# Attention of a two-layer trunk: query tiles 4 to 7 by pairs, with the values as fp32r high and low columns

## The chip, the core and the metric

The kernel runs on one core of a Trainium2 chip. The metric is the device time of one launch in microseconds (us), lower is better. The program's engines are named as in the profile: PE is TensorE, DVE is VectorE, ACT is ScalarE, POOL is GpSimd, SP is SyncE, which here only issues DMAs.

## The reference

The model has two layers over x (1 x 1024 x 1024, float32): an even one with latent attention beside an S5 state-space branch, and an odd one with chunked gated linear attention. Each ends in x <- LayerNorm(alpha * x + y). The change lies in the even layer and at its end:

```python
def block(args):                       # 8 blocks of 128 queries, 8 heads, q and k of 64 + 32, v of 64
    qn, qp, i = args
    s = (jnp.einsum('bqhd,bkhd->bhqk', qn, k_nope)
         + jnp.einsum('bqhr,bkr->bhqk', qp, k_pe)).astype(jnp.float32) * scale
    causal = k_idx[None, :] <= q_idx[:, None]
    s = jnp.where(causal, s, -jnp.inf)
    p = jax.nn.softmax(s, axis=-1).astype(v.dtype)
    return jnp.einsum('bhqk,bkhd->bqhd', p, v)

y = jax.nn.gelu(y)                                      # s5_layer, 256 wide
y = y * jax.nn.sigmoid(y @ w_glu + b_glu)

o_mla = mla_attention(...) * jax.nn.silu(g_mla)         # even_layer, 512 wide
o_s5 = s5_layer(...) * jax.nn.silu(g_s5)
return jnp.concatenate([o_mla, o_s5], axis=-1) @ w_out
```

All inputs and the output are float32.

## The kernel before

All 1024 tokens are cut in 8 tiles of 128 (P = 128, NT = 8). TensorE has two kinds of product here. An fp32 product is one instruction that the hardware runs as passes of its own. An "fp32r" product uses operands that were split beforehand in a high part (a copy rounded to fp32r) and a low part (raw minus high), and three passes: hi x hi, lo x hi, hi x lo. The big projections are of the second kind; the attention's scores, transposes and values are of the first.

Attention goes through `heads`, 64 pairs (i, h) of query tile and head, tile by tile. For each, with i + 1 blocks of 128 keys:
- "s": scores. TensorE multiplies the turned queries of the head (qTt, 96 x 128, as weights) with the turned keys kT, up to 512 columns per instruction, and adds the causal mask (L1963, L1967). Tiles 0 to 3 use one of four PSUM banks, tiles 4 to 7 two pairs of banks in turn.
- VectorE takes the negative maximum out of PSUM (negmax, L1623), ScalarE the exponential with the row sum as accumulator (prob, L1209).
- "pt": TensorE transposes prob block by block (L1885) into banks 4 and 5, at most four blocks a bank. VectorE copies the first bank of a head to SBUF, ScalarE the second one (both `copy_probs`, L696), into four slots of probT.
- "av": TensorE multiplies with probT as weights and 64 columns of V as the moving operand (L2100), into bank 7, where the 8 heads of a tile lie side by side.

At a tile's last head VectorE takes the reciprocals of the sums (L1682), scales the output (L1684) and multiplies the gate (L1688, into the gate's own buffer). "OT": TensorE transposes the gated tile, and VectorE copies it to OT (L1691). "q" and "qT" compute and transpose the queries of later tiles in between; GpSimd turns their rotary part.

Beside it VectorE computes the sigmoid of the S5 gate in 16 pieces (`sigmoid_gate`, L1646 to L1648: 1 + exp, reciprocal, product; the exponentials ran on ScalarE), and GpSimd splits w_out (rows 128 k, k = 0 to 5): k = 1 to 3 while the queries of tiles 2 to 4 pass, k = 0, 4, 5 behind tile 7's, then w_gk and the first head of wqk, a weight of the next layer.

Then the output projection: "z0" for tile i multiplies the split w_out with the mixed tile (4 blocks of OT, 2 of gs5), whose high parts ScalarE casts (`mix_hi_tile`, L1228, L1229) and whose low parts VectorE subtracts (`mix_lo_tile`, L1654, L1656). For each tile the layer norm follows: VectorE adds the residual and takes the statistics, ScalarE the root, GpSimd applies ln_g and ln_b (L1030, L1031), TensorE turns the result (zn). The transposes of tile 7's gated output, "OT" of tile 7, stand after the product of tile 0.

The order of the work on every engine is the order in which `attention_steps` yields its steps; each engine's program walks through the same list and takes its own part of each step. A plan hands PSUM banks from job to job: a job claims its bank when the reader of the job before has freed it, and "filled" and "drained" are waits on the semaphores of a job's writer and reader. SP's DMAs stand in one list too; each waits for what frees its buffer.

## Time and profile before

| | |
|---|---|
| median of 3 runs | 893.23 us (891.41 to 896.03) |
| the profiled execution | 895.35 us, span of its core 893.3 us, mean granted clock 0.986 |
| PE busy | 852.8 us, 95% of the span, 4360 instructions |
| DVE busy | 590.0 us, 66% |
| ACT busy | 326.9 us, 37% |
| POOL busy | 248.1 us, 28% |
| DMA | 64.21 MB, mean 72 GB/s |

The span is the time between the first and the last instruction of the profiled execution; the time of the execution lies 2.1 us above it. Matmuls overlap in a trace: a row's duration is longer than the distance to the next one's start, and it is the distance that tells the engine's rate. The granted clock is given as a share of full speed, 2.4 GHz; the engine's other level is 1.2 GHz. A row with xN stands for N instructions that follow one another. L12 is line 12 of the kernel.

### The profile page before, as it was taken

What the parts mean: (1) busy time and instruction counts of PE and PEld (TensorE: products, weight loads), DVE (VectorE), ACT (ScalarE), POOL (GpSimd) and SP (SyncE); (2) the same over time, 40 slices, a digit from 0 to 9 for tenths busy, and PEclk for the clock granted to TensorE, in tenths of its full rate; (3) what the DMA queues carried; (4) which work ended last, traced back from release to release, by engine and by line L of the source; (5) the groups of instructions that cost most, each with busy time, mean ns of one, the idle gap of its engine ahead of it and who ended that gap; (6) DMA issues with size and microseconds to landing.
All of it is one profiled execution on the core that took longest, in us unless ns stands there. A gap on an engine that the chain in (4) does not pass through costs nothing.

```text
span 893.3 us, 12333 instructions
## 1 busy us (share of the span) xinstructions
PE 852.8 (95%) x4360; PEld 691.8 (77%) x4360; DVE 590.0 (66%) x961; ACT 326.9 (37%) x626; POOL 248.1 (28%) x251
## 2 busy tenths in 40 slices
PE   7999999999999999999998999999799999999995
PEld 5899777756677777787875888888588888888884
DVE  6988688557687775637871443488986667544543
ACT  6251514654333434412222645045243446111210
POOL 2000001415211111506656231005753013332243
PEclk9999999999999999999998899999999999999998
DMA  9101164220000111032223110236334322111111
GB/s 335 35 20 30 48 118 96 50 74 1 1 2 1 39 34 48 1 105 108 95 95 118 47 48 1 83 94 191 123 102 140 105 74 103 38 61 48 48 59 59
DMA packets 40685, 64.21 MB, mean 72 GB/s; under 512 B 8256, under 2 KB 21824, under 8 KB 40608
## 3 DMA queue, kind: packets, MB, share of 16 engines
q1 hardware_dynamic: 40624, 63.42, 23.2%
q8 instruction: 35, 0.57, 0.3%
q14 instruction: 26, 0.21, 0.1%
HBM read 52.33 MB, written 9.44 MB: 69 GB/s over the span
## 4 chain that ended last, share of the span: by engine, by line
PE 72%; DVE 17%; ACT 3%; DMA 3%; issue 2%; SPq 1%; POOL 1%; DVEq 0%; ACTq 0%; POOLq 0%
PE psum L1876 39%; PE psum L2177 14%; PE psum L2100 6%; PE psum L1963 6%; PE psum L1885 6%; PE psum L1911 1%; DVE vg_lo L1748 1%; DVE probT L696 1%; DMA wgs_raw<-even_w_in_dram 1%; DVE x_hi_raw L1779 1%; DVE x_lo_raw L1780 1%; DMA xT_raw<-x_cols_dram 1%; DMA ln_gb<-ln_b_dram 1%; DVE qTt L1617 1%; ACT xT_hi L1117 1%
## 5 line engine op out<-in xcount | busy, mean ns | idle before, releaser
L2177 PE MATMUL psum<-vg_hi,x1T_hi 128*128 128x512 f32 x208 | 82.0, 394 | 4.9 <-DVE vg_lo L1748 4.2
L2177 PE MATMUL psum<-vg_hi,x1T_lo 128*128 128x512 f32 x208 | 81.7, 393 | 0.0
L2177 PE MATMUL psum<-vg_lo,x1T_hi 128*128 128x512 f32 x208 | 81.6, 392 | 0.0
L2100 PEld LDWEIGHTS psum<-V,probT 128*128 128x128 f32 x576 | 69.3, 192 | 12.4 <-issue 8.4
L1209 ACT ACTIVATE prob<-psum,negmax 128x128 f32<-128x128 f32 (+7 forms) x64 | 47.4, 741 | 82.0 <-DVE negmax L1623 74.4
L2100 PE MATMUL psum<-V,probT 128*128 128x64 f32 x576 | 74.5, 275 | 0.5 <-DVE rot L1684 0.3
L1963 PE MATMUL psum<-kT,qTt 96*128 96x512 f32 (+3 forms) x192 | 72.5, 487 | 1.2 <-DVE YT L713 1.2
L1623 DVE TENSOR_REDUCE negmax<-psum 128x1 f32<-128x128 f32 (+7 forms) x64 | 48.5, 758 | 28.2 <-PE psum L1967 26.7
L696 DVE COPY probT<-psum 128x512 f32<-128x512 f32 (+3 forms) x64 | 37.8, 591 | 22.4 <-PE psum L1885 20.7
L2177 PEld LDWEIGHTS psum<-vg_hi,x1T_hi 128*128 128x128 f32 x208 | 39.3, 189 | 15.3 <-DVE vg_lo L1748 6.2
L1876 PE MATMUL psum<-x1T_lo,wqk_hi 128*128 128x512 f32 x128 | 50.8, 397 | 0.0
L1876 PE MATMUL psum<-x1T_hi,wqk_hi 128*128 128x512 f32 x128 | 50.8, 397 | 0.0
L1876 PE MATMUL psum<-x1T_hi,wqk_lo 128*128 128x512 f32 x128 | 50.8, 397 | 0.0
L1876 PE MATMUL psum<-w_out_hi,Y1T_hi 128*128 128x512 f32 x128 | 50.6, 395 | 0.0
L1876 PE MATMUL psum<-w_out_hi,Y1T_lo 128*128 128x512 f32 x128 | 49.9, 390 | 0.0
L1876 PE MATMUL psum<-w_out_lo,Y1T_hi 128*128 128x512 f32 x128 | 49.8, 389 | 0.0
L1963 PEld LDWEIGHTS psum<-kT,qTt 96*128 96x128 f32 x192 | 32.4, 190 | 20.0 <-issue 16.8
L2177 PEld LDWEIGHTS psum<-vg_hi,x1T_lo 128*128 128x128 f32 x208 | 39.4, 189 | 8.3
L2177 PEld LDWEIGHTS psum<-vg_lo,x1T_hi 128*128 128x128 f32 x208 | 39.3, 189 | 8.1
L1399 DVE SCALAR_TENSOR_TENSOR SG<-V,psum 128x512 f32<-128x512 f32 x16 | 11.0, 688 | 49.8 <-PE psum L1876 49.8
L1096 POOL TENSOR_TENSOR SG<-SG,ln_gb 128x1024 f32<-128x1024 f32 (+1 forms) x8 | 18.2, 2277 | 92.1 <-DVE SG L1406 92.1
L1885 PE MATMUL psum<-ident,prob 128*128 128x128 f32 x288 | 42.4, 274 | 0.8 <-ACT prob L1209 0.5
(393 smaller groups left out, 2087.5 us busy)
## 6 DMA issues: line engine op xcount, KB each, us to landing
vg_piece<-odd_w_in_dram SPq DMA_DIRECT2D x60, 256.0 KB, 3.3
wqk_raw<-odd_w_in_dram SPq DMA_DIRECT2D x8, 512.0 KB, 5.3
x_res<-x_dram SPq DMA_DIRECT2D x8, 512.0 KB, 4.0
x_scratch<-zn SPq DMA_DIRECT2D x8, 512.0 KB, 2.9
w_out_raw<-odd_w_out_dram SPq DMA_DIRECT2D x4, 1024.0 KB, 5.0
V<-x_scratch SPq DMA_DIRECT2D x8, 512.0 KB, 4.4
out_dram<-SG SPq DMA_DIRECT2D x8, 512.0 KB, 2.9
xT_raw<-x_cols_dram SPq DMA_DIRECT2D x7, 512.0 KB, 7.6
```

Of the source, the lines that this page charges most:

```text
L696: ins = engine.activation(dst, src, ACT.Copy) if engine is nc.scalar else engine.tensor_copy(dst, src)
L1096: step(pool.tensor_tensor(z, z, g, ALU.mult))
L1117: step(act.activation(xT_hi[:, k, s], xT_raw[k][:, s], ACT.Copy), xT_hi_set)
L1209: step.frees(act.activation(prob[:, place:place + (i + 1) * P], src, ACT.Exp, bias=negmax[:, n % 4:n % 4 + 1], accum_out=rsum[:, i % 2, h: ...
L1399: step.frees(vec.scalar_tensor_tensor(zt[:, s], res[:, s], ALPHA, bank(job, i, n), ALU.mult, ALU.add), (job, i, n))
L1617: step.frees(vec.tensor_copy(qTt[:, n % 2, 4 * half:4 * half + 4, :], bank("qT", n, half)[0:QK, :].rearrange("p (h t) -> p h t", h=4)), (" ...
L1623: step(vec.tensor_reduce(negmax[:, n % 4:n % 4 + 1], scores(n)[0], AX_X, ALU.max, negate=True), max_set)
L1876: mm = pe.matmul(out, lhsT, rhs, start=(k == 0), stop=(k == len(pairs) - 1))
L1885: mm = pe.transpose(bank(*job)[0:rows, k * P:k * P + cols], block_in, identity[0:cols, 0:cols])
L1963: mm = pe.matmul(psum[:, slot + part, 0:c1 - c0], qTt[:, i % 2, h, :], kT[:, h, c0:c1], start=True, stop=not diag, skip_group_check=diag)
L2100: mm = pe.matmul(bank("o", i)[:, h * VD:(h + 1) * VD], lhsT, rhs, start=(k == 0), stop=(k == len(pairs) - 1))
L2177: mm = pe.matmul(bank(*job), lhsT, rhs, start=(k == 0 and j == 0 and product not in ADDS_TO), stop=(k == 3 and j == len(pairs) - 1), skip_ ...
```

## The change

For query tiles 4 to 7 the list `heads` now takes two tiles together: (4,0), (5,0), (4,1), (5,1) and so on, then tiles 6 and 7. A pair (tile 2p, tile 2p+1) of one head is a step m. Its probabilities are transposed as before, but each transposed bank is split in fp32r: ScalarE casts the high part (L1304), VectorE subtracts the low part from PSUM (L1777). Both tiles' blocks of the same keys stand side by side in a cell (hi and lo, 4 blocks x 2 tiles x 128 queries); there are three cells. "pv" replaces "av": the weights are 128 columns of V, the head's 64 value columns as fp32r high parts and the same 64 as low parts, and the moving operand is 256 columns of the cell, first the high ones, then the low ones. So two passes a block give (hi + lo) x (hi + lo), with the high columns' product in one half of the partitions and the low columns' in the other; ScalarE copies one half out (`output_parts`), VectorE adds them (`output_gated`). The last block of a pair serves the second tile alone, with 128 columns. The output comes out turned (value x query), so the tile is not transposed; instead the gate is: VectorE scales the gate by the reciprocals of the sums (`gate_scaled`), TensorE transposes it ("gT"), ScalarE copies it to gateT, and VectorE multiplies. This happens once for every two heads of a pair of tiles.

V is stored per block of keys as [high | two raw or low columns | high] (V_raw names the middle as float32). GpSimd casts the high columns of all blocks behind the turning of tile 2's queries, with the low columns of blocks 4 to 7 there, and the low columns of blocks 0 to 3 once tile 3's last values are done. The first pv waits for them.

Tiles 0 to 3 go one by one as before, but VectorE alone copies their probT. Further:
- ScalarE computes the S5 gate's sigmoid by its own function; VectorE multiplies it in four pieces at heads 10 to 16.
- The queries of tiles 4 to 7 are computed and transposed at other steps (QUERIES, TURNS), with a second buffer qt.
- GpSimd splits w_gk and then the six pieces of w_out in one block behind tile 7's queries; wqk's first head is loaded at the end of the attention and split between the layer norms of tiles 2 and 3. ln_g and ln_b are loaded behind it, once the last output is gated.
- "OT" of tile 7 behind the first product is gone.

The diff, cut to its core:

```diff
-        heads = [(i, h) for i in range(NT) for h in range(H)]
+        heads = [(i, h) for i in range(4) for h in range(H)]
+        FIRST = len(heads)
+        heads += [(2 * p + t, h) for p in range(2, NT // 2) for h in range(H) for t in range(2)]
...
             for n, (i, h) in enumerate(heads):
+                if n > FIRST and n % 2 == 0 and n > FIRST + 1:
+                    yield "pv", (n - FIRST) // 2 - 1
                 yield "pt", n
...
-                if n:
+                if 0 < n <= FIRST:
                     yield "av", n - 1
-                if h == 4 and i:
+                if n < FIRST and h == 4 and i:
                     yield "OT", i - 1
-            yield "av", len(heads) - 1
+                if n == FIRST + 2:
+                    yield "OT", 3
+                if n in OUTPUT_TURNS:
+                    yield "gT", OUTPUT_TURNS.index(n)
+            yield "pv", STEPS - 1
+            yield "gT", PAIRS - 1
             yield "z0", 0
-            yield "OT", NT - 1
...
# ScalarE, at "pt"
-                    if 4 <= n + 1 < len(heads):
+                    if 4 <= n + 1 < len(heads) and (n < FIRST or n % 2 == 0):
                         exponentials(n + 1)
-                    for number, first, blocks in pt_jobs[heads[n]][1:]:
-                        copy_probs(act, step, number, first, blocks)
+                    for number, first, blocks in pt_jobs[heads[n]] if n >= FIRST else ():
+                        plan.filled(act, ("pt", number))
...
+                        (hi, _), source = prob_blocks(n, number, first, blocks)
+                        step(act.activation(hi, source, ACT.Copy), prob_hi_set)
+                    if FIRST < n + 1 < len(heads) and n % 2:
+                        exponentials(n + 1)
+                    if n in OUTPUT_TURNS:
+                        output_parts(OUTPUT_TURNS.index(n))
...
# VectorE, at "pt"
+                    if n in OUTPUT_TURNS:
+                        gate_scaled(OUTPUT_TURNS.index(n))
+                    if n - 1 in OUTPUT_TURNS:
+                        output_gated(OUTPUT_TURNS.index(n - 1))
...
+                            vec.wait_ge(prob_hi_set, number + 1 - FIRST)
+                            (hi, lo), source = prob_blocks(n, number, first, blocks)
+                            step.frees(vec.tensor_tensor(lo, source, hi.bitcast(F32), ALU.subtract), ("pt", number))
-                    if 24 <= n < 56 and n % 2 == 0:
-                        sigmoid_gate((n - 24) // 2)
+                    if n in (10, 12, 14, 16):
+                        sigmoid_gate((n - 10) // 2)
...
# TensorE
+                elif what == "pv":
+                    p, h = 2 + n // H, n % H
+                    job = ("o_odd" if h % 2 else "o_even", n // 2)
...
+                    for k in range(2 * p + 2):
...
+                        t0 = int(k == 2 * p + 1)
+                        for part, cell in enumerate(cells[(2 * n + k // 4) % 3]):
+                            mm = pe.matmul(bank(*job)[:, c0 + t0 * P:c0 + 2 * P],
+                                           V[k][:, h // 2, 2 * (h % 2):2 * (h % 2) + 2, :].rearrange("p s d -> p (s d)"),
+                                           cell[:, k % 4, t0:2, :].rearrange("p t q -> p (t q)"),
...
+    def gate_scaled(j):
+        p, k = 2 + j // 4, j % 4
+        plan.drained(vec, ("s", FIRST + 4 * j + 3))
...
+        step(vec.reciprocal(inverses, sums))
+        block_ = gate[:, k, 2 * p * P:2 * (p + 1) * P].rearrange("p (t h d) -> p t h d", t=2, h=2)
+        step(vec.tensor_tensor(block_, block_, inverses.unsqueeze(3).to_broadcast([P, 2, 2, VD]), ALU.mult), gated)
+
+    def output_gated(j):
+        p, k = 2 + j // 4, j % 4
+        plan.drained(vec, ("o_even", j))
+        src = bank("o_odd", j)
+        step(vec.tensor_tensor(o_sum[0:VD, :], src[0:VD, 0:2 * P], o_low[0:VD, :], ALU.add))
+        step(vec.tensor_tensor(o_sum[VD:P, :], src[VD:P, 2 * P:4 * P], o_low[VD:P, :], ALU.add))
+        plan.drained(vec, ("gT", j))
+        step.frees(vec.tensor_tensor(OT[:, k, 2 * p * P:2 * (p + 1) * P], o_sum[:, :], gateT[j % 2][:, :],
+                                     ALU.mult), ("o_odd", j))
...
# GpSimd
-                if 2 <= i < 5:
-                    w_out0_split_slice(i - 1, 0, 48)
+                if i == 2:
+                    for j in (4, 5, 6, 7, 0, 1, 2, 3):
+                        plan.drained(pool, ("vp", j))
+                        step(pool.tensor_copy(V[j][:, :, 0:4:3, :], V_raw[j][:, :, 1:3, :]))
+                        if j >= 4:
+                            value_low(j)
+                if i == 5:
+                    plan.filled(pool, ("o", 3))
+                    for j in range(4):
+                        value_low(j)
...
+                if i in (2, 3):
+                    wqk_split_part(0, i - 2)
...
# SP, at tile 1 of the output projection's residual loads
-                    sp.wait_ge(gated, NT)
+                    plan.filled(sp, ("o_odd", PAIRS - 1))
+                    wqk_load(0)
+                    plan.drained(sp, ("o_odd", PAIRS - 1))
```

How this moves instructions, first on ScalarE in tile 7 of the kernel before. An exponential and one copy of a bank follow each other, head by head:

```order
L1209 ACTIVATE prob,rsum<-psum,negmax 128x1024
L696 ACTIVATE probT<-psum 128x384
L1209 ACTIVATE prob,rsum<-psum,negmax 128x1024
L696 ACTIVATE probT<-psum 128x512
L1209 ACTIVATE prob,rsum<-psum,negmax 128x1024
L696 ACTIVATE probT<-psum 128x512
L1209 ACTIVATE prob,rsum<-psum,negmax 128x1024
```

And on ScalarE in the pair of tiles 6 and 7 now, from the exponential of tile 6's head (896 columns) on; probT_hi_89, 91 and 93 are the three cells:

```order
L1262 ACTIVATE prob,rsum<-psum,negmax 128x896
L1262 ACTIVATE prob,rsum<-psum,negmax 128x1024
L1304 ACTIVATE probT_hi_89<-psum 128x4x128
L1304 ACTIVATE probT_hi_91<-psum 128x3x128
L1286 ACTIVATE o_low<-psum 64x256
L1287 ACTIVATE o_low<-psum 64x256
L1315 ACTIVATE gateT_204<-psum 128x256
L1304 ACTIVATE probT_hi_89<-psum 128x4x128
L1304 ACTIVATE probT_hi_91<-psum 128x4x128
L1262 ACTIVATE prob,rsum<-psum,negmax 128x896
L1262 ACTIVATE prob,rsum<-psum,negmax 128x1024
```

Two exponentials stand together now, four copies of high parts behind them, of which in every second step two are preceded by the output's three copies.

On VectorE in tile 7 before, with tile 6's normalisation in the middle:

```order
L1623 TENSOR_REDUCE negmax<-psum 128x1
L696 COPY probT<-psum 128x512
L1623 TENSOR_REDUCE negmax<-psum 128x1
L1682 RECIPROCAL rinv<-rsum 128x8
L1684 TENSOR_TENSOR rot<-psum,rinv 128x512
L1688 TENSOR_TENSOR gate<-gate,rot 128x512
L696 COPY probT<-psum 128x512
L1623 TENSOR_REDUCE negmax<-psum 128x1
```

And on VectorE in tiles 6 and 7 now, a step with output work (probT_lo_90, 92 and 94 are the cells' low parts):

```order
L1698 TENSOR_REDUCE negmax<-psum 128x1
L1727 RECIPROCAL rinv<-rsum 128x2x2
L1729 TENSOR_TENSOR gate<-gate,rinv 128x256
L1777 TENSOR_TENSOR probT_lo_90<-psum,probT_hi_89 128x4x128
L1777 TENSOR_TENSOR probT_lo_92<-psum,probT_hi_91 128x3x128
L1698 TENSOR_REDUCE negmax<-psum 128x1
L1737 TENSOR_TENSOR o_sum<-psum,o_low 64x256
L1738 TENSOR_TENSOR o_sum<-psum,o_low 64x256
L1740 TENSOR_TENSOR gate<-o_sum,gateT_204 128x256
L1777 TENSOR_TENSOR probT_lo_90<-psum,probT_hi_89 128x4x128
L1777 TENSOR_TENSOR probT_lo_92<-psum,probT_hi_91 128x4x128
L1698 TENSOR_REDUCE negmax<-psum 128x1
```

A head's single copy has become two subtractions, which stand between the maxima; the scaling of the gate stands before the first head's, the gating of the output before the second head's.

On GpSimd before, from the last turning of queries (qt) to the first layer norm (zn):

```order
L706 TENSOR_TENSOR qt<-work 128x8x16
L993 CAST w_out_hi<-w_out_raw_184 128x1024
L994 TENSOR_TENSOR w_out_lo_190<-w_out_raw_184,w_out_hi 128x1024
L993 CAST w_out_hi<-w_out_raw_188 128x1024
L994 TENSOR_TENSOR w_out_lo_194<-w_out_raw_188,w_out_hi 128x1024
L993 CAST w_out_hi<-w_out_raw_189 128x1024
L994 TENSOR_TENSOR w_out_lo_195<-w_out_raw_189,w_out_hi 128x1024
L993 CAST w_gk<-w_gk_raw 128x8x16
L994 TENSOR_TENSOR w_gk<-w_gk_raw,w_gk 128x8x16
L993 CAST wqk_hi<-wqk_raw 128x1024
L994 TENSOR_TENSOR wqk_lo<-wqk_raw,wqk_hi 128x1024
L993 CAST wqk_hi<-wqk_raw 128x1024
```

And now, from the same place, the rows from the fourth piece of w_out on:

```order
L1026 CAST w_out_hi<-w_out_raw_213 128x1024
L1027 TENSOR_TENSOR w_out_lo_219<-w_out_raw_213,w_out_hi 128x1024
L1026 CAST w_out_hi<-w_out_raw_214 128x1024
L1027 TENSOR_TENSOR w_out_lo_220<-w_out_raw_214,w_out_hi 128x1024
L1026 CAST w_out_hi<-w_out_raw_209 128x1024
L1027 TENSOR_TENSOR w_out_lo_215<-w_out_raw_209,w_out_hi 128x1024
L1079 TENSOR_TENSOR zn<-zn,ln_gb 128x512
L1080 TENSOR_TENSOR zn<-zn,ln_gb 128x512
L1079 TENSOR_TENSOR zn<-zn,ln_gb 128x512
```

The split of wqk no longer stands ahead of the layer norms of tile 0; the pieces of w_out are six in a row.

## Rows read from the trace of the kernel before

**Rows 1.** The page, part 4: the last chain, its share of the span by engine.

```profile
PE 72%; DVE 17%; ACT 3%; DMA 3%; issue 2%; SPq 1%; POOL 1%; DVEq 0%; ACTq 0%; POOLq 0%
```

**Rows 2.** Windows: us; busy us (instructions) of PE, PEld, DVE, ACT, POOL; PEclk; DMA; GB/s.

```profile
262.70:388.10 125.40, 124.96 (x839) 99.08 (x839) 88.69 (x125) 50.63 (x102) 23.53 (x24) 1.00 0.09 28
407.40:463.90 56.50, 56.50 (x266) 46.55 (x267) 42.06 (x64) 13.61 (x27) 37.99 (x28) 0.97 0.29 103
```

**Rows 3.** Timeline of PE in tile 7: start us, us, engine line op out<-in xcount.

```profile
359.30 1.88 PE L1963 MATMUL psum<-kT,qTt 96*128 96x512 f32 x4
361.07 1.95 PE L2100 MATMUL psum<-V,probT 128*128 128x64 f32 x16
362.86 1.05 PE L1885 MATMUL psum<-ident,prob 128*128 128x128 f32 x8
363.74 1.88 PE L1963 MATMUL psum<-kT,qTt 96*128 96x512 f32 x4
...
365.46 0.22 PE L1967 MATMUL psum<-causal_bias,ident_b 128*128 128x128 bf16 x1
```

**Rows 4.** Chain of waits in tile 4 (281 to 294 us): start us, us, what.

```profile
282.34 1.08 PE psum L1963 x4
...
283.48 1.11 PE psum L2100 x10
```

**Rows 5.** Timeline of PE in the input projection, two passes 32 apart.

```profile
83.75 0.35 PE L1911 MATMUL psum<-wa_hi,xT_lo 128*128 128x416 f32 x1
...
89.73 0.34 PE L1911 MATMUL psum<-wa_lo,xT_hi 128*128 128x416 f32 x1
```

**Rows 6.** Timeline of ACT in tile 7.

```profile
363.59 1.11 ACT L1209 ACTIVATE prob<-psum,negmax 128x1024 f32<-128x1024 f32 x1 [3.32 <-DVE negmax L1623]
...
364.82 0.60 ACT L696 ACTIVATE probT<-psum 128x512 f32<-128x512 f32 x1
```

**Rows 7.** Timeline of DVE in tile 7; in brackets idle us before, releaser.

```profile
362.28 1.23 DVE L1623 TENSOR_REDUCE negmax<-psum 128x1 f32<-128x1024 f32 x1
363.56 0.69 DVE L696 COPY probT<-psum 128x512 f32<-128x512 f32 x1
365.79 1.22 DVE L1623 TENSOR_REDUCE negmax<-psum 128x1 f32<-128x1024 f32 x1 [1.54 <-PE psum L1967]
```

**Rows 8.** DVE's groups by form: xcount | busy us, mean ns | idle us before, releaser.

```profile
L1647 DVE RECIPROCAL SGL<-SGL 128x128 f32<-128x128 f32 x16 | 15.2, 953 | 0.6
L1623 DVE TENSOR_REDUCE negmax<-psum 128x1 f32<-128x768 f32 x8 | 7.7, 958 | 3.5 <-PE psum L1967 3.3
```

**Rows 9.** ACT's groups by form.

```profile
L1209 ACT ACTIVATE prob<-psum,negmax 128x768 f32<-128x768 f32 x8 | 7.2, 902 | 17.0 <-DVE negmax L1623 17.0
```

**Rows 10.** POOL's groups by form.

```profile
L994 POOL TENSOR_TENSOR w_out_lo<-w_out_raw,w_out_hi 128x1024 fp32r<-128x1024 f32 x6 | 14.1, 2352 | 0.5
L994 POOL TENSOR_TENSOR wv_lo<-wv_raw,wv_hi 128x512 fp32r<-128x512 f32 x4 | 5.1, 1274 | 0.3
```

**Rows 11.** One line, L1688: xcount, ns shortest/median/longest, first and last start us, forms.

```profile
L1688 DVE TENSOR_TENSOR gate<-gate,rot x8: 692/693/1746, 206.9 to 389.8; 128x512 f32<-128x512 f32 x8
```

**Rows 12.** Timeline of ACT: end of tile 0, and output projection.

```profile
197.87 0.49 ACT L1182 ACTIVATE qt<-psum 128x384 f32<-128x384 f32 x1 [3.81 <-PE psum L1876]
...
401.24 1.28 ACT L1251 ACT_TABLE_LOAD   x1 [15.81 <-DVE stat L1403]
```

**Rows 13.** Timeline of DVE at the output projection's start.

```profile
397.06 0.69 DVE L1691 COPY OT<-psum 128x512 f32<-128x512 f32 x1 [6.55 <-PE psum L1885]
```

**Rows 14.** Timeline of POOL there.

```profile
405.98 1.32 POOL L1031 TENSOR_TENSOR zn<-zn,ln_gb 128x512 f32<-128x512 f32 x1
```

**Rows 15.** Timeline of PE there.

```profile
407.36 0.66 PE L1885 MATMUL psum<-ident,zn 128*128 128x128 f32 x4 [2.19 <-POOL zn L1031]
```

**Rows 16.** DMA issues: out<-in queue op xcount, KB each, median us to landing.

```profile
wqk_raw<-odd_w_in_dram SPq DMA_DIRECT2D x8, 512.0 KB, 5.3
ln_gb<-ln_b_dram SPq DMA_DIRECT2D x2, 512.0 KB, 6.0
```

More of the change, by code:

```diff
@@ L211, in hybrid_trunk @@
         prob = at("prob", D1, [P, 2 * S])
-        probT = at("probT", RD + 17920, [P, 4, 512])
+        cells = [[at(f"probT_{part}{c}", RD + 14336 + 2048 * c + 1024 * n, [P, 4, 2, P], F32R)
+                  for n, part in enumerate(("hi", "lo"))] for c in range(3)]
         cT = at("cT", D2, [P, 3, S])
@@ L465, in hybrid_trunk @@
                 count += 1
+        STEPS = (len(heads) - FIRST) // 2
+        PAIRS = STEPS // 2
+        cell_users = [(m, g) for m in range(STEPS) for g in range(2)]
         SHORT = [n for n, (i, h) in enumerate(heads) if i < 4]
@@ L1950, in queries_turn @@
                 pe.wait_ge(q_turned, n + 1)
-                turned(("qT", n, half), [(qt[:, h, :], QK) for h in range(4 * half, 4 * half + 4)])
+                turned(("qT", n, half), [(qt[n % 2][:, h, :], QK) for h in range(4 * half, 4 * half + 4)])
             def score(n):
```

207 lines of the change are left out of this document (135 added, 72 removed).

## The prediction, made before the changed kernel was run

> **What bounds the kernel now.** I read the chain of waits first: TensorE holds 72% of it [rows 1], so the question is where an instruction of TensorE can be saved and who is late when it is. Then the stages: from the first transposes of query tile 4 (262.7 us) to the first product of the output projection (388.1) TensorE is busy 124.96 of 125.40 us, VectorE 88.69, ScalarE 50.63 [rows 2]. One head of tile 7 shows why. Scores begin at 359.30, values at 361.07, transposes of the next head at 362.86, the next scores at 363.74 [rows 3]: 1.77 + 1.79 + 0.88 = 4.44 us without a gap. The values are 8 blocks of 0.224 us, each two passes with the probabilities as weights and 64 columns moving; the transposes are 0.11 us a block. A head of tile 4 has 1.08 us of scores and 1.11 us of values [rows 4], that is 0.215 and 0.222 us a block; the mask between them costs 0.06. So a head of tile 4, 5, 6, 7 takes 2.75, 3.3, 3.9, 4.45 us, and two heads 6.16 us (tiles 4 and 5) or 8.35 us (6 and 7). Eight of each are 116.1 us; four halves of queries (5.2), six of their transposes (2.6) and the transposes of outputs (1.8) bring it to 125.7, as measured.
>
> **The values on TensorE.** 128 heads' worth of blocks go: 8 x (5+6+7+8) = 208 of 0.224 us, 46.6 us. In their place a pair of tiles shares each block of values: two passes, high and low probabilities, over 256 columns, and the last block two over 128. An f32r pass over 416 columns takes (89.73 - 83.75)/32 = 0.187 us [rows 5], 0.0135 more than 416/2.4 GHz; by the same surplus 256 columns take 0.120. No row has f32r with so few columns. From below it is bounded by the 0.112 us of a value pass now [rows 3], from above by what an fp32 product over 256 columns takes, 2 x 0.215 = 0.43 [rows 4]. I take 0.120, since the 416-column row is of the same kind, and 0.11 for 128 columns. A round (one head of both tiles) then costs TensorE, scores + transposes + values: tiles 4, 5: 2.49 + 1.21 + 1.42 = 5.12 us; tiles 6, 7: 3.34 + 1.65 + 1.90 = 6.89 us. Were TensorE still the bound, 8 x (1.04 + 1.46) = 20 us would be won.
>
> **What is late next.** The order of the changed kernel shows a ring through VectorE and ScalarE. ScalarE runs both exponentials of a round, then four copies of high parts; VectorE runs low(first tile), maximum, low(second tile), maximum. The exponential of the second tile waits for VectorE's last maximum, the high copies stand behind it, and the low parts behind them. Durations [rows 6 to 9]: exponential over 1024 columns 1.11, with its accumulator read 1.23 to the next instruction's start (363.59 to 364.82), over 768 by the same 0.12 about 1.02; a copy over 512 0.60; a maximum 1.23 (1024) and 0.96 (768), so 0.27 us per 256 columns; a low part out of PSUM 0.69 (512), and 0.56, 0.42, 0.29 for three, two, one blocks by that slope. A VectorE step costs 0.04 more to the next. Between engines I read 0.08 (maximum ends 363.51, exponential starts 363.59) and 0.27 from TensorE's issue to a reader (the mask's at 365.46 + 0.06, the maximum at 365.79).
> With A the end of the second maximum, tiles 6, 7: exponential A+0.08 to 1.31, high part to 1.91, low part 1.99 to 2.68; second group 2.72 to 3.28; maximum over 896 from 3.32; the second tile's two low parts 4.45 to 5.87 (its transposes could start at 2.76, its high part ends at 4.05, so they are ready); its successor's scores end on TensorE at 3.80 + 1.77 = 5.57, readable at 5.85; maximum 5.91 to 7.14. **7.14 us a round** against 8.35 before. Tiles 4, 5: low part ends 2.47, one-block low part and maximum over 640 to 3.70, but the second tile's high part is there only at 2.47 + 0.08 + 0.44 + 0.25 + 0.60 + 0.08 = 3.92; low parts to 5.11, maximum over 768 to **6.07 us a round** against 6.16. TensorE (5.12, 6.89) waits inside both rings.
> The sum from tile 4's first transposes:
> - 8 rounds of 6.07 and 7 of 7.14, and 0.6 for the first maxima of tiles 6, 7: 99.2 us.
> - Output steps, after every second round. ScalarE's two partial copies and the gate copy fit beside VectorE; the reciprocal and scaling of the gate fit in VectorE's 2 us of waiting after A. Three VectorE steps over 256 columns (3 x 0.46 = 1.38) do not: they stand before the second tile's low parts. Three times 1.38 - 0.22 and four times 1.38: 9.0 us.
> - Four copies of turned queries on VectorE, 0.73 each: 2.9 us.
> - The start. Tile 3's normalisation (about 1.8 us on VectorE) falls in round 1: +1.6. In round 2 two halves of queries (1.29 each) and tile 3's output transposes stand before scores, and the first values wait for four low parts of GpSimd, 1.27 us each [rows 10], that begin when tile 3 is done: +3.1. Together 4.7.
> - Low parts of the first two mixes (0.73 + 0.42 each), hidden under TensorE before: 2.3 us.
> - From A of the last round to the first output product: low part at 4.8, values 1.9, gate transposes 0.2: 7.0 us.
> - VectorE's SBUF steps beside GpSimd: 0.9 us. The row is tile 6's gate product, which took 1.75 us while GpSimd split weights; the median of the eight is 0.69 [rows 11].
> Sum 126.0 against 125.4: **+0.6 us**. The 20 us stay in the waits.
> The Trainium skill (SBUF — State Buffer, section "SBUF: two separate sides") speaks against this change more strongly: a VectorE step with two SBUF inputs and a GpSimd step shut each other out of a shared port for a whole instruction. The trace agrees as far as it goes, with the one product of 1.75 us. By the rule every output step during the six weight splits, now one block of about 21 us (w_out_lo 2.35 each), could wait up to 2.35 us [rows 10]; some three output rounds lie there, so the sum would be up to 5 us higher instead of 0.9.
>
> **Before and after that stage.** The gate of the S5 branch becomes a Sigmoid: two table loads of 1.28 us each [rows 12]. The first lies in the time in which ScalarE waits for TensorE's products, the second before the exponential of head 4, where ScalarE had idled 3.81 us [rows 12]: cost 0.1 (at most 2.6). Sixteen reciprocals of 0.95 us leave VectorE [rows 8]; TensorE waited for few of them, since the stage of tiles 0 to 3 gives VectorE short copies, and what turns up there is paid back by tile 5's queries, whose turning moves into it. I take 0 for tiles 0 to 3, bounds -2 and +2.6.
> At the projection's start the kernel now turns tile 7's output after the first product: VectorE copies it at 397.06 [rows 13] before the layer norm may begin, a table load at 401.24 follows [rows 12], GpSimd ends at 407.30 [rows 14], and TensorE, 2.19 us idle, restarts at 407.36 [rows 15], 19.3 us after 388.1. After this wait the granted clock falls: over the 56.5 us from 407.4 it is 0.97, over the attention before it 1.00 [rows 2]. That is a few us at the lower of its two levels, 1.2 instead of 2.4 GHz, and costs 0.03 x 56.5 = 1.7 us; the two decimals allow 1.4 to 2.0, I take 1.5. In the changed kernel the output tile needs no turning there, so VectorE starts when the first half of the product is ready: 8.3 (product) + 2.1 (VectorE) + 1.7 (ScalarE with its table load) + 1.1 + 3.1 (GpSimd) = 16.3 us, when TensorE has just ended the second product at 16.5 us: no wait, no slow passes. **-4.3 us**. It needs ln_gb: issued about 2.3 us after the first product's start behind a megabyte of wqk (landings 6.0 and 5.3 us) [rows 16], so there at about 12, wanted at 13. The split of wqk's first head, moved among the layer norms of tiles 2 and 3 (3.5 us each), fits: GpSimd has 5.3 us of work in 9.1 us a tile.
>
> Sum: 0.6 - 4.3 = -3.7 us. The profiled execution took 895.35 us (span 893.3 and 2.1 around it), so it would take 891.6; it lies 2.1 above the median of the three runs, 893.23, and from that I forecast **889.5 us**.
>
> **Rivals.**
> 1. TensorE stays the bound. For it: it is busy in 99% of the stage, and my ring has sixteen hand-overs estimated to a tenth. If they close faster, rounds cost 5.2 and 7.0, the output steps hide, and the stage ends at about 8 x 12.2 + 7.4 (queries) + 5 (start, tail) = 110: -15 and -4.3, 874 us; half of it gives 882. Against it: VectorE's own four steps and ScalarE's exponential are rows.
> 2. Slower: the clock. In an output round of tiles 4, 5 TensorE idles 6.07 + 1.16 - 5.23 = 2.0 us, as long as the wait of 2.19 us after which it fell [rows 15]; one fall costs 1.5 us, and if it comes back into each of some ten such rounds the stage gains 15 us: 889.5 + 15 = 904. It decides once one wait is as long as that one. Against it: the 2.0 us are spread over two or three waits.
> 3. An f32r pass over 256 columns costs more. From 0.17 us on TensorE's round of tiles 6, 7 passes the ring with its output steps; at 0.215 the stage takes 129 us (893 in all), at 0.43 it takes 170 (934).
> 4. ln_gb or the GpSimd queue is late and the projection starts no sooner: 893.5 us.
>
> **How the numbers follow.** Forecast 0.54, its own range 885 to 895; rival 1 0.24; rival 2 0.12; rival 3 0.05; rival 4 0.05. About 0.5% (4.5 us, below 888.8 or above 897.7) is what a measurement can tell. Faster: 0.24 and 0.21 of the forecast's own, 0.45. Slower: 0.12 and 0.03 of rival 3, 0.15. The rest, 0.40, is the same. Range 876 to 901: below it lies the full form of rival 1, above it the full form of rival 2 and rival 3.
>
> **What would show it.** In the changed trace: value passes 0.12 us apart; in rounds of tiles 6, 7 about 7.1 and 8.5 us in turn, in tiles 4, 5 about 6.1 and 7.2; TensorE waiting for probT low parts and prob, VectorE idle about 2 us before the first low part of a round; the first transposes of zn 16.5 us after the first product, with clock 1.00. I am wrong if TensorE is 98% busy in the stage (rival 1), if its clock is below 0.95 there (rival 2), or if passes stand 0.17 us apart or more (rival 3).

## The result, and the profile after

The changed kernel took 899.58 us in the median of 6 runs (897.23 to 902.61), the kernel before 895.11 us beside it: 1.0053 times, 95% interval 1.0032 to 1.0074. It is 0.5% slower, where 889.5 us and "the same or faster" were forecast. The profiled execution took 902.61 us, span 900.9, mean granted clock 0.98 (before: 895.35, 893.3, 0.986).

What the ring through VectorE and ScalarE was said to cost came out nearly to the digit. This is a round of tiles 6 and 7 without output steps, then one with them, on VectorE (start us, us, line, operation; in brackets idle time before, and what ended it):

```profile
352.69 1.28 DVE L1777 TENSOR_TENSOR probT_lo<-psum,probT_hi 128x512 fp32r<-128x512 f32 x2 [2.02 <-ACT probT_hi L1304]
...
356.59 1.22 DVE L1698 TENSOR_REDUCE negmax<-psum 128x1 f32<-128x1024 f32 x1
...
362.28 0.42 DVE L1737 TENSOR_TENSOR o_sum<-psum,o_low 64x256 f32<-64x256 f32 x1
...
365.10 1.22 DVE L1698 TENSOR_REDUCE negmax<-psum 128x1 f32<-128x1024 f32 x1
```

The second maximum ends at 357.81 and at 366.32; the one before, 2.02 us ahead of 352.69, at 350.67: rounds of 7.14 and 8.51 us, forecast 7.14 and 8.5. The same ring on ScalarE: the exponential begins 0.08 us after 357.81, the high parts follow it at 359.13, and VectorE's low part follows them at 359.83:

```profile
357.89 1.12 ACT L1262 ACTIVATE prob<-psum,negmax 128x1024 f32<-128x1024 f32 x1 [1.10 <-issue]
```

The passes of the values cost what was taken, 0.12 us apart over 256 columns (columns: start us, us, line, operation; TensorE):

```profile
271.96 0.28 PE L2226 MATMUL psum<-probT_hi,V 128*128 128x256 f32 x1
272.08 0.28 PE L2226 MATMUL psum<-probT_lo,V 128*128 128x256 f32 x1
```

And the chain of waits answers [rows 1] with TensorE 12 points lower and VectorE 7 higher:

```profile
PE 60%; DVE 24%; issue 6%; ACT 5%; DMA 3%; POOL 2%; SPq 1%; DVEq 0%; ACTq 0%; POOLq 0%
```

What was not forecast stands on TensorE. These are its waits at four places (in brackets). Between them stand tile 4's first transposes at 264.61, the first product of the output projection at 393.63 and the first transposes of zn at 410.46 (timeline of TensorE):

```profile
209.62 2.82 PE L1985 MATMUL psum<-w_uq,cT 128*128 128x384 f32 x4 [1.91 <-DVE qTt L1692]
...
264.61 0.72 PE L1994 MATMUL psum<-ident,prob 128*128 128x128 f32 x5
...
387.21 1.90 PE L1994 MATMUL psum<-ident,prob 128*128 128x128 f32 x8 [3.01 <-DVE probT_lo L1777]
...
393.63 0.70 PE L1985 MATMUL psum<-w_out_hi,mix_hi 128*128 128x512 f32 x1
...
410.46 0.66 PE L1994 MATMUL psum<-ident,zn 128*128 128x128 f32 x4
...
466.80 0.66 PE L1994 MATMUL psum<-ident,zn 128*128 128x128 f32 x4 [0.89 <-POOL zn L1080]
...
745.14 0.66 PE L1994 MATMUL psum<-ident,KS 128*128 128x128 f32 x4 [2.44 <-POOL KS L1124]
```

At 209.6, 387 and 745 us, behind three of these waits, the clock falls. Windows of the changed kernel (us; busy us and instructions of PE, PEld, DVE, ACT, POOL; granted clock; DMA share; GB/s):

```profile
200.00:220.00 20.00, 17.80 (x104) 12.93 (x103) 14.48 (x29) 8.04 (x27) 16.57 (x24) 0.91 0.00 2
264.60:393.60 129.00, 111.29 (x644) 80.95 (x644) 91.43 (x144) 77.84 (x155) 32.29 (x30) 0.98 0.08 29
380.00:400.00 20.00, 15.33 (x78) 13.30 (x77) 10.04 (x17) 6.41 (x13) 0.00 (x0) 0.83 0.44 133
740.00:760.00 20.00, 17.56 (x90) 15.61 (x89) 11.77 (x24) 10.96 (x27) 8.07 (x13) 0.83 0.25 90
```

The second row answers to [rows 2]: the stage is 129.0 us instead of 125.4, TensorE is busy in 111.3 of it (before 124.96), VectorE in 91.4. The other rows are the falls: 0.09, 0.17 and 0.17 of 20 us, that is 1.8, 3.4 and 3.4 us of clock. The kernel before lost its 1.8 us at 400 to 420 and nothing at these three. Both kernels also lose some 5 us at 480 to 500 (clock 0.74 in either) and 1.7 us at 630 to 640 (0.83 in either), and waits of about 2 us stand ahead of those falls too; in the kernel before (timeline of TensorE):

```profile
482.31 0.40 PE L1876 MATMUL psum<-x1T_hi,w_gk 128*32 128x512 f32 x1 [2.03 <-DVE x1T_lo L1707]
...
489.87 0.97 PE L1876 MATMUL psum<-low_parts,gk_parts 96*128 96x512 f32 x2 [1.91 <-DVE low_parts L1662]
```

Over these windows the profiled execution of the changed kernel lost 15.5 us of clock and that of the kernel before 8.7: 6.8 of the 7.3 us between them.

Counted along the two traces the change is 1.9 us late at tile 4's first transposes, 5.6 at the first output product, 2.7 at the w_gk product that waits for the last tile's low parts (482.31 before, 485.00 now), 4.4 at the transposes of 745 and 7.6 at the end.

### The profile page after: what moved, and what is told of

It reads as the page before. It is cut to its first block, busy times and chain, and to the rows that moved or that the text cites. A ratio compares the mean times of both kernels' runs of the same rounds, so it can differ in the third digit from the quotient of the medians.

```text
span 900.9 us, 12127 instructions
## 1 busy us (share of the span) xinstructions
PE 843.2 (94%) x4168; PEld 677.2 (75%) x4168; DVE 593.6 (66%) x972; ACT 358.5 (40%) x684; POOL 265.2 (29%) x267
## 4 chain that ended last, share of the span: by engine, by line
PE 60%; DVE 24%; issue 6%; ACT 5%; DMA 3%; POOL 2%; SPq 1%; DVEq 0%; ACTq 0%; POOLq 0%
PE psum L1985 36%; PE psum L2308 14%; PE psum L1994 3%; DVE probT_lo L1777 3%; PE psum L2020 3%; PE psum L2072 2%; DVE negmax L1698 2%; PE psum L2205 1%; ACT probT_hi L1304 1%; DVE vg_lo L1857 1%; ACT prob L1262 1%; DVE xT_lo L1496 1%; DMA ln_gb<-ln_b_dram 1%; DMA wgs_raw<-even_w_in_dram 1%; DVE x_hi_raw L1888 1%
## 5 line engine op out<-in xcount | busy, mean ns | idle before, releaser
L1262 ACT ACTIVATE prob<-psum,negmax 128x640 f32<-128x640 f32 (+5 forms) x64 | 47.5, 742 | 46.0 <-issue 29.5
L1698 DVE TENSOR_REDUCE negmax<-psum 128x1 f32<-128x640 f32 (+5 forms) x64 | 48.5, 758 | 19.2 <-PE psum L2076 17.5
L1777 DVE TENSOR_TENSOR probT_lo<-psum,probT_hi 128x512 fp32r<-128x512 f32 x64 | 37.8, 591 | 29.6 <-ACT probT_hi L1304 28.0
L1079 POOL TENSOR_TENSOR zn<-zn,ln_gb 128x512 f32<-128x512 f32 x16 | 23.3, 1455 | 105.5 <-DVE zn L1482 104.8
L1994 PEld LDWEIGHTS psum<-ident,prob 128*128 128x128 f32 x288 | 33.2, 148 | 13.4 <-issue 12.9
```

What stands on the lines that cost most here:

```text
L1079: step(pool.tensor_tensor(zn[:, i % 2, s], zn[:, i % 2, s], ln_gb[:, 0, s], ALU.mult))
L1262: step.frees(act.activation(prob[:, place:place + (i + 1) * P], src, ACT.Exp, bias=negmax[:, n % 4:n % 4 + 1], accum_out=rsum[:, i % 4, h: ...
L1698: step(vec.tensor_reduce(negmax[:, n % 4:n % 4 + 1], scores(n)[0], AX_X, ALU.max, negate=True), max_set)
L1777: step.frees(vec.tensor_tensor(lo, source, hi.bitcast(F32), ALU.subtract), ("pt", number))
L1994: mm = pe.transpose(bank(*job)[0:rows, k * P:k * P + cols], block_in, identity[0:cols, 0:cols])
```

## The experiments

The theory (A): the rings are as forecast; what was lost beyond them is TensorE's clock after waits of about 2 us and more, which the change made longer. Its rivals are told with each run. "The stage" is from tile 4's first transposes to the first output product, read in each run's profile; ratios are against the kernel before in the same series.

**The changed kernel again.**

> The changed kernel once more, unchanged, beside the next three on one chip. Theory A (waits of about 2 us bring the clock down, at 209.6 and 745 us in some executions and not in others, at 384 us in all): 1.003 to 1.007 times before; the first output product 129.0 us after tile 4's first transposes again, with the clock at 0.8 to 0.9 from 380 to 400 us. Rival E (the difference found was the luck of its six runs): 1.000 to 1.002.

1.0066 (1.0042 to 1.009). Stage 128.6 us, clock 0.66 from 390 to 400; at 209 us it fell too, at 742 us, after 2.24 us of waiting, it did not. Rival E is out.

The span and the mean granted clock of every execution were taken too, and they tell more than single profiles can. The median clock is 0.984 in both series of the changed kernel (13 executions) and 0.990 in the 28 of the kernel before beside the second. One minus the clock, times the span, is 14.4 us against 8.9: 5.5 us more, where the times differ by 5.2. Span times clock, an estimate of the time at full clock, is 883.8 and 883.4 us for the changed kernel and 882.6 for the kernel before. So apart from the clock the change is worth about nothing, neither a loss of 5 us nor a gain of 3.7.

**A filler in the last round.** On TensorE, behind head 62's transposes:

```diff
+                    if n == 62:
+                        for _ in range(24):
+                            pe.transpose(psum[:, 0, 0:P], ident[:, :], ident[:, :])
```

> The changed kernel with 24 transposes of the identity (0.11 us each, 2.6 us) written to a PSUM bank that nobody reads, on TensorE ahead of the last head's transposes, where it waited 3.01 us for VectorE (384.2 to 387.2). No other engine's work or wait is touched. Theory A (the clock fell because of that wait, and the fall costs the tail about 3.4 us): granted clock 1.00 from 380 to 400 us instead of 0.86 and 0.80, the first output product 2.5 to 3.5 us sooner after tile 4's first transposes (125.5 to 126.5 us instead of 129.0), the time 3 us shorter, 1.002 times that of before. Rival B (the tail is long because of the hand-overs between VectorE and ScalarE, the clock costs nothing there since TensorE is waiting anyway): 128.5 to 129 us, 1.005. Rival C (the clock falls from something else than an idle TensorE): clock still below 0.9.

0.9996 (0.998 to 1.0012), 5 us less than without it. Stage 126.87 us (264.23 to 391.10), and its window of 20 us is at full clock:

```profile
380.00:400.00 20.00, 17.64 (x112) 15.62 (x113) 9.93 (x18) 5.96 (x12) 0.00 (x0) 1.00 0.52 158
```

Work that computes nothing made the kernel faster: theory A for this place. From the last maximum to the first product it is now 7.2 us, as forecast (7.0), where the changed kernel had 9.3. But the stage gave only 2.2 us of the 5 and lies 0.4 us above the range given. The rest is clock as well: over the executions its median is 0.989 instead of 0.984, worth 4.6 us, and span times clock is 883.0, as in the kernel before. In this profile the clock falls neither at 209 nor near 743 us; why a filler at 384 us should spare the later place no run shows.

**Low parts of the first mixes moved off the last maximum.**

```diff
+                    if n in (60, 62):
+                        mix_lo_tile((n - 60) // 2)
                     for number, first, blocks in pt_jobs[heads[n]]:
...
-                    if n in (59, 61):
-                        mix_lo_tile((n - 59) // 2)
```

> The changed kernel with VectorE's low parts of the first two mixed tiles moved from behind the low parts of heads 59 and 61 to ahead of those of heads 60 and 62, so behind the maximum and into VectorE's 2 us of waiting for ScalarE. Theory A: the last maximum begins 1.15 us sooner, TensorE waits 1.9 instead of 3.01 us in the last round, the stage is 1.1 us shorter for the second and about as much for the first (126.7 to 127.9 instead of 129.0), and 3 us more if the shorter wait no longer brings the clock down; 1.000 to 1.003. Rival B (these steps hide behind ScalarE): 129.0, 1.005.

TensorE's wait was 1.82 us and the stage 126.4 us, 2.6 shorter and 0.3 below the range given. The clock fell all the same (0.82 and 0.84 from 380 to 390 and from 390 to 400), and the ratio was 1.0048 (1.0028 to 1.0067), above the 1.000 to 1.003 expected: that profile also lost more clock at 210 (0.71), and the median clock of its executions is 0.982. The move is real (span times clock 881.4 us, some 2 less than without it), but a shorter wait alone did not save the clock.

**The split of the values held back until tile 0 is gated.**

```diff
                 if i == 2:
+                    pool.wait_ge(gated, 1)
                     for j in (4, 5, 6, 7, 0, 1, 2, 3):
```

> The changed kernel with one more wait on GpSimd: the split of the values' high and low columns begins only when tile 0's output is gated, so that it does not run beside that gate product. Theory A (the product took 1.51 us instead of 0.69 because GpSimd ran beside it; TensorE therefore waited 1.91 us at 209.6 and its clock fell): product 0.7 us, wait about 1.1 us, clock 1.00 from 208 to 214, tile 4's first transposes at 262.0 to 262.8 instead of 264.6; 2 to 2.6 us shorter in all. Rival B (the product is slow for another reason): 1.5 us and everything as it was. Rival C (the wait shortens but the clock falls all the same): 0.8 us shorter.

The gate product took 0.69 us, where it had taken 1.51 beside GpSimd and 0.99 in the kernel before, there beside a split of w_out. TensorE waited 1.09 us without a fall. But what stands behind the split on GpSimd, the turning of tile 3's queries, came later, and TensorE waited for that (timelines of VectorE in the changed kernel and in this run, then of TensorE in this run):

```profile
206.88 1.51 DVE L1794 TENSOR_TENSOR gate<-gate,rot 128x512 f32<-128x512 f32 x1
```

```profile
206.33 0.69 DVE L1795 TENSOR_TENSOR gate<-gate,rot 128x512 f32<-128x512 f32 x1
```

```profile
222.66 0.91 PE L1995 MATMUL psum<-ident,qt 128*96 128x128 f32 x4 [3.18 <-POOL qt L738]
```

Clock 0.83 from 220 to 230, ratio 1.0075 (1.005 to 1.01). The cause of the long product is shown, the remedy moved the wait. The product agrees with the Trainium skill (SBUF — State Buffer, "SBUF: two separate sides"): a VectorE step with two SBUF inputs and a GpSimd step take turns on a port.

**One pass of the values.** The products of the low parts of the probabilities left out:

```diff
-                        for part, cell in enumerate(cells[(2 * n + k // 4) % 3]):
+                        for part, cell in ((0, cells[(2 * n + k // 4) % 3][0]),):
```

> The changed kernel without the products of the low parts of the probabilities in tiles 4 to 7 (the values' passes halved, the output loses that part); VectorE and ScalarE do all that they did. It takes 0.71 us (tiles 4, 5) and 0.95 us (6, 7) of TensorE's work out of each of the 16 rounds, 13 us in all. Theory A (the rounds are bound by the ring through VectorE and ScalarE): stage 127 to 129.5 us instead of 129.0, the idle time of TensorE 11 us longer, time 0 to 2 us shorter, unless longer waits bring the clock down (then up to 10 us longer). Rival D (TensorE's work is still the bound): stage 13 us shorter, 0.991.

0.9998 (0.9978 to 1.0019), stage 127.7 us, with a further fall at 320 to 340 us, behind a wait of 2.02 us. TensorE's 13 us brought 1.3 us of stage, far from rival D; the median fell more than theory A said, by 5 us instead of 0 to 2. The pair with the filler follows.

> The changed kernel with the 24 transposes at the end and without the products of the low parts of the probabilities: the clean partner of the run in which VectorE's subtractions were cut as well (stage 116.3 us). Theory A (TensorE's work is worth next to nothing, VectorE's is worth its whole length): stage 124.5 to 126.5 us, so that 8 to 10 us of the 10.6 us won there are VectorE's. Rival D (TensorE's 13 us made most of it): 116 to 120 us.

Stage 126.66 us, against 126.87 with both passes. The fall at 320 to 340 us came again and cost some 1.7 us of it, for which the range given was missed by 0.2 on its high side; without it the 13 us of TensorE's work would be worth 1.9 us of stage. 1.0006 (0.9984 to 1.0028).

**VectorE's low parts cut as well.**

```diff
-                            step.frees(vec.tensor_tensor(lo, source, hi.bitcast(F32), ALU.subtract), ("pt", number))
+                            step.frees(vec.tensor_tensor(lo[:, 0:1, :], source[:, 0:1, :], hi[:, 0:1, :].bitcast(F32),
+                                                         ALU.subtract), ("pt", number))
```

> The changed kernel with the 24 transposes at the end, without the products of the low parts of the probabilities (as in the run with one pass, which took 13 us of TensorE's work out), and with VectorE's subtraction of low parts cut to one block of 128 columns a bank (0.29 instead of 0.69, 0.56 or 0.42 us; the output loses the low parts). It takes 0.9 us (tiles 4, 5) and 1.5 us (6, 7) out of VectorE's share of a round, 19 us in all. Theory A (the ring goes through VectorE's steps): the stage from tile 4's first transposes to the first output product falls from 126.9 us to 108 to 117 us. Rival H (the ring's time is ScalarE's copies and the hand-overs, VectorE's subtractions lie beside them): 123 us or more.

0.9895 (0.9876 to 0.9914), stage 116.25 us. Windows of the stage in the run before this and in this one; only VectorE's busy time (third of the busy columns) differs much, 91.4 and 74.2 us. The first has the fall in it, the second has none:

```profile
263.26:389.92 126.66, 102.00 (x557) 69.01 (x556) 91.36 (x144) 77.74 (x155) 32.21 (x30) 0.99 0.07 25
```

```profile
264.64:380.89 116.25, 99.05 (x556) 67.97 (x556) 74.17 (x144) 77.73 (x155) 32.30 (x30) 1.00 0.07 26
```

17 us off VectorE are 10.4 us of stage, 8.7 with the first window's fall taken off; 13 us off TensorE were 0.2, or 1.9 with it taken off. The ring is VectorE's in the main.

**ScalarE's high parts ahead of the second exponential** (with the filler):

```diff
-                    if 4 <= n + 1 < len(heads) and (n < FIRST or n % 2 == 0):
+                    if 4 <= n + 1 < len(heads) and n <= FIRST:
                         exponentials(n + 1)
...
-                    if FIRST < n + 1 < len(heads) and n % 2:
+                    if FIRST < n and n + 1 < len(heads):
                         exponentials(n + 1)
```

> The changed kernel with the 24 transposes at the end, and ScalarE's order in tiles 4 to 7 changed: the high parts of a pair's first tile ahead of the exponential of the second one, where ScalarE waited for VectorE's maximum. VectorE and TensorE keep their order. Theory A (the first low part of a round waits 2 us for its high part behind that exponential) by itself gives rounds of 6.9 us and a stage of 120 to 124 us instead of 126.9. But the high parts then wait for the transposes, which on TensorE stand behind the values of the round before (1.9 us): by that count a round of tiles 6 and 7 takes 7.8 us and the stage 128 to 133 us. I expect the second, 1.003 to 1.006 times before; rival I (VectorE is the only engine that counts): 120 to 124 us, 0.994.

Stage 127.7 us, 1.0005 (0.9987 to 1.0023): rival I is out, my 128 was just too high, and so was the ratio of 1.003 to 1.006. Rounds of tiles 6 and 7 are 7.7 and 8.1 us in turn (transposes at 346.50, 354.62, 362.35): evener than 7.25 and 8.4, and in sum no shorter. VectorE's one wait of 2.02 us became two of 1.50 and 0.76, and TensorE's transposes now wait for the exponential (0.38 and 0.61 us).

**A filler in the kernel before**, ahead of the first transposes of zn:

```diff
+                if i == 0 and half == 0:
+                    for _ in range(16):
+                        pe.transpose(psum[:, 7, 0:P], ident[:, :], ident[:, :])
                 pe.wait_ge(x1_set, 2 * i + half + 1)
```

> The kernel before with 16 transposes of the identity (1.8 us) into an unused PSUM bank on TensorE, ahead of the first transposes of zn, where it waited 2.19 us for GpSimd. Theory A (that wait brought the clock down for some us, worth 1.5 us in the sum of the prediction): clock 1.00 from 400 to 420 us instead of 0.91 and 0.92, the second transposes of zn 24.0 us after the first output product instead of 25.5; 0.998 times before. Rival C (the clock falls from something else): 25.5 us, 1.000.

The second transposes came 23.94 us after the first product (before 25.51), the wait was 0.47 us, the clock 1.00. The time was 1.0001 (0.9985 to 1.0018): the trace bears out the 1.5 us, the medians do not tell them apart from none.

**A second filler** beside the 24 transposes:

```diff
                 if what == "q":
+                    if n == (3, 0):
+                        for _ in range(12):
+                            pe.transpose(psum[:, 0, 3 * P:4 * P], ident[:, :], ident[:, :])
                     queries(*n)
```

> The changed kernel with the 24 transposes at the end of the attention (as measured: 0.9996) and 12 more (1.3 us) ahead of the queries of tile 3, where TensorE waits 1.9 us for VectorE. Theory A (in the executions in which the clock falls there, it costs 1.9 us, and it falls because of the wait): clock never below 1.00 from 200 to 230 us, tile 4's first transposes not later than 264.3, 0.5 to 1.5 us shorter than with the filler at the end alone, 0.9985. Rival F (the fall there is rare and costs nothing in the median): 0.9996.

Tile 4's first transposes at 263.23, clock 1.00 there and at the end, 0.9982 (0.9965 to 0.9999). The interval holds rival F's 0.9996 too; the median clock of the executions, 0.993 against 0.989 with the one filler, speaks for theory A. Of the eleven profiles in which TensorE waits 1.90 or 1.91 us at that place, seven show the fall and four do not.

**The split of wqk's first head moved on GpSimd** (both with the 24 transposes). First one half:

```diff
-                if i in (2, 3):
-                    wqk_split_part(0, i - 2)
+                if i in (2, 5):
+                    wqk_split_part(0, i // 5)
```

> The changed kernel with the 24 transposes at the end of the attention, and the second half of the split of wqk's first head moved on GpSimd from the layer norm of tile 3 to that of tile 5. Theory A (a tile with a split takes GpSimd 10.2 us where TensorE needs 9.1, and two in a row leave TensorE 0.9 us idle at 467): no wait of TensorE for zn at 464, w_gk's first product 1.0 to 1.3 us sooner after the first output product (90.2 us instead of 91.4), 0.998. Rival G (the wait comes from VectorE's conflicts with GpSimd, whatever the order): 91.4 us, 0.9996.

No gain: wait 1.05 us, 91.3 us from the first output product to the w_gk product behind the last tile's low parts, 1.0 (0.9981 to 1.0019). Then both halves:

```diff
-                if i in (2, 3):
-                    wqk_split_part(0, i - 2)
+                if i == NT - 1:
+                    wqk_split_head(0)
```

> The changed kernel with the 24 transposes at the end, and the split of wqk's first head behind the last layer norm of the projection. Theory A (TensorE's wait of 0.9 to 1.05 us for zn near 464 us comes from the splits ahead of it): no wait there, 90.3 us instead of 91.3 from the first output product to w_gk's first product, and nothing lost later, since that head's products begin 20 us later; 0.9985. Rival J (TensorE has to wait once for the chain through VectorE and GpSimd at the end of the projection, whatever else GpSimd does, because it no longer waited at the start of it): 91.3 us, 0.9996.

1.012 (1.0103 to 1.0136). I had misread the order: that head's first products stand right behind the last transposes of zn, behind one w_gk product, not 20 us later, and TensorE waited for them:

```profile
478.40 0.80 PE L1985 MATMUL psum<-x1T_hi,wqk_hi 128*128 128x512 f32 x1 [11.39 <-POOL wqk_lo L1027]
```

Ahead of that, the last transposes of zn ran without a wait, all eight in one piece, as in the kernel before:

```profile
462.14 1.11 PE L1994 MATMUL psum<-ident,zn 128*128 128x128 f32 x8
```

So the 0.9 us are the splits' doing, whichever tile they stand in; rival J is out for the wait, and the remedy was worse than it.

**A filler near 743 us**, none in the attention:

```diff
                 if what == "kT1":
+                    if i == 2:
+                        plan.claim(pe, ("kT1", i))
+                        for _ in range(10):
+                            pe.transpose(bank("kT1", i)[:, 0:P], ident[:, :], ident[:, :])
                     pe.wait_ge(ks_set, i + 1)
```

> The changed kernel, without any filler in the attention, with 10 transposes of the identity (1.1 us) on TensorE ahead of the transposes of KS near 743 us, where it waits 2.2 to 2.4 us for GpSimd in the profiled executions of the changed kernel (0.9 to 1.1 us in those of before) and the clock then falls in three of four. Theory A (that fall is a part of what the median lost, since the filler at the end of the attention won 5 to 6 us in the median and only 2.2 us in its stage): no clock below 1.00 from 735 to 765 us, 1.003 to 1.0045 times before instead of 1.0053 and 1.0066. Rival K (the late fall is an accident of the profiled executions): 1.005 to 1.007.

1.0031 (1.0013 to 1.0048) instead of 1.0053 and 1.0066: some 2 to 3 us, so the late fall was part of the loss. The intervals overlap, but the clocks agree: their median is 0.987 instead of 0.984 over 12 executions, worth 2.8 us, with span times clock unchanged at 884.0. TensorE's wait was 1.34 us behind the filler, the clock 1.00 from 735 to 765 us.

**The version that beats both**: 14 transposes in the last round, 12 ahead of tile 3's queries, and the low parts moved as in the second experiment.

> The changed kernel with 14 transposes at the end (1.5 us, since the wait there is 1.8 us in this order), 12 ahead of tile 3's queries, and the low parts of the first two mixed tiles moved as before. Theory A: clock 1.00 from 200 to 230 and from 380 to 400 us, the stage 124.5 to 125 us, 0.9955 times before (0.9982 with the two fillers alone). Rival F (in the executions without a fall the moved steps lie beside ScalarE's work): stage 126.9 us, 0.998.

890.81 us, 0.9964 (0.9948 to 0.9979), the stage 124.53 us:

```profile
263.69:388.22 124.53, 110.10 (x659) 80.13 (x658) 91.43 (x144) 77.75 (x155) 32.26 (x30) 1.00 0.08 28
```

The move is worth 2.3 us of stage here, about as in the second experiment, and now the time shows it, since the clock holds: its median is 0.9895, as in the kernel before, and span times clock is 880.1 us against 882.5.

## Why the prediction was wrong, by its own steps

- **The rounds** (7.14 and 8.5 us, 6.1 and 7.2): right. Tiles 4 and 5 had 6.22, 7.98, 6.94, 7.23 us between second transposes from 292.7 on; the 7.98 and the 6.94 each hold a copy of turned queries (0.72), which the sum had apart. That most of TensorE's gain stays in the waits is shown by the three stages 126.87, 126.66 and 116.25. Two slips had no weight: the blocks that go are those of 32 heads, not 128, and the first term adds up to 99.1.
- **The stage** (126.0): 126.9 at full clock, 129.0 as it ran. The failed term is the last one, "From A of the last round to the first output product". Taken as 7.0, it was 7.2 with the filler and 9.3 without. I had counted the wait and not what it does: with no next scores to fill it, TensorE idles 3.01 us, and 6.8 us of what follows run at 1.2 GHz (clock 0.83 from 380 to 400). The 0.9 us for VectorE's steps beside GpSimd were about right and lay in VectorE's own waits: of the eight scalings of the gate six took 0.42 us and two, beside the splits, 1.23 and 0.64. The 5 us that the port could have cost there did not come.
- **Rival 2** (the clock, 0.12) named the mechanism at the wrong place. The output rounds' waits are at most 1.36 us in the changed kernel and nothing falls there. "It decides once one wait is as long as that one" was the right test; I put it to the rounds and not to the ends of the stage.
- **Tiles 0 to 3** (0, bounds -2 and +2.6): +1.9 in the profiled execution. I weighed reciprocals and table loads, and forgot GpSimd's new work, whose split of the values stretches the gate product from 0.99 to 1.51 us; TensorE's wait grows from 1.39 to 1.91, after which the clock falls in seven of eleven profiles. Where it doesn't, tile 4 begins only 0.4 to 0.7 us later than before, counted from the products at 151 us; with the fall it is 1.8 to 3.3. The rule about the port that I had weighed for the output steps decided here.
- **The projection's start** (-4.3): the restart came 16.8 us after the first product (forecast 16.5), without wait or slow passes behind it: this step held. But 0.89 us are waited for zn at 466, so to the w_gk product the gain is 94.2 - 91.4 = 2.8 us. The claim that GpSimd has 5.3 us of work in 9.1 and that the split fits was too tight: its tiles with a split are 10.2 us apart (zn at 423.47, 433.64, 443.83).
- **Behind the change** I assumed nothing. TensorE's wait for KS, 0.93 us before, was 2.2 to 2.4 us in four of the five profiles in which ln_b's transfer took 7.8 to 8.0 us (1.34 behind the filler in the fifth) and 0.9 to 1.3 in the others (6.5 to 6.9 us). The changed kernel's filler there is worth 2 to 3 us. Why the transfer is slower is open: it was issued at 733.5 to 736.6 us in the five, earlier in nearly all others, but at 742.5 in one in which it took 6.7 us.

Summed over the two profiled executions, in which the change is 7.6 us late at the end instead of 3.7 early: 1.9 us in tiles 0 to 3, 3.1 in the stage, 1.4 in the projection, 4.9 behind it. Over all executions: forecast -3.7 us, measured +4.7 to +5.9, and -1.6 (0.9982) with fillers at two places. The clocks of all executions account for 5.5 us, so the clock is the whole of the wrong sign. They do not account for the whole of the miss: without the 1.5 us that I took back from the clock the forecast was -2.2 us, and at full clock the changed kernel measures about 1 us more than the one before. That remainder is about what the longer waits last by themselves, for the gate product (0.5), for zn (0.9) and for KS (1.5).

## What to carry to other kernels

When work is taken off TensorE and the path goes on through other engines, look where its waits now run together, first at the ends of a stage, where no next tile fills them: many of 0.3 to 1.4 us cost only themselves, one near 2 us or more can cost as much again in clock. Filler transposes are a cheap test of that, and here a cheap remedy. When an engine off the path gets new work, look up what runs beside it on VectorE, not only whether it fits its own budget.

## What the runs showed of the hardware

- The granted clock fell after all six last-round waits of 1.82 to 3.72 us, after none that fillers had cut to 1.20 or less, and after seven of eleven waits of 1.9 us at 209 us. Near 2 us it is a matter of the execution.
- The same holds where both kernels wait: at 480 to 500 us, after waits of 2.03 and 1.90, the clock fell in 12 of 16 profiles, at 632 us, after 2.01 to 2.06, in 15 of 16; at 305 us, after 2.07 and 2.08, in neither of two. Every fall between 200 and 880 us in the sixteen profiles began during a wait of 1.82 us or more, or less than 3 us behind its end.
- An fp32r pass over 256 columns costs 0.12 us, one over 128 columns 0.06 (start to start, 273.80 to 273.86; from the second to the transposes behind it 0.11), where I had taken 0.11.
